# A hybrid decoder layer: the down projection in five groups instead of three, its product sums partly copied by ScalarE, and the first up pair in another order

## What is computed

```
h = h + xo @ p["w_xo"]
u, gv = jnp.split(rmsnorm(h, p["norm_ffn_g"]) @ p["w_up"], 2, axis=-1)
u, new_ffn_buf = causal_dwconv(u, ffn_buf, p["ffn_conv_w"])      # 3 taps
h = h + (jax.nn.silu(u) * gv) @ p["w_down"]
...
y_prompt = rmsnorm(hp, final_norm_g)
```

## Time and profile before

| quantity | value |
|---|---|
| time, median of 3 runs | 1997.17 us (1996.79 to 1999.99) |
| time of the profiled execution | 1992.7 us |
| its span | 1990.9 us |
| mean granted TensorE clock | 0.981 |
| PE, PEld busy | 1817.4 us (91%), 1699.2 us (85%) |
| DVE, ACT, POOL busy | 1206.2, 694.0, 748.6 us |
| first up product, first down product, end part | at 1227.12, 1704.83, 1951.93 us |

### The profile page before, as it was taken

One profiled execution on the slowest core, in us unless ns is written; L12 is line 12 of the kernel. 1 busy time (PEld: TensorE's weight loads), 2 busy tenths in 40 slices (PEclk: granted clock), 3 DMA queues, 4 the chain that ended last, 5 costly groups with the idle time before them and its releaser, 6 DMA issues. The chain is left out here.

```text
span 1990.9 us, 35520 instructions
## 1 busy us (share of the span) xinstructions
PE 1817.4 (91%) x14041; PEld 1699.2 (85%) x14041; DVE 1206.2 (61%) x1506; ACT 694.0 (35%) x1292; POOL 748.6 (38%) x621
## 2 busy tenths in 40 slices
PE   6988899999999899999999796999999999699997
PEld 5866799987887788998988596999999999698887
DVE  6877366754554231564142448788888888856655
ACT  6055326643222103412032526333333333424333
POOL 3411033331211123755664022444445454344444
PEclk9999999999999999999999998999999999799999
DMA  4311111110102021422222201332222332534422
GB/s 187 91 38 40 38 43 37 38 61 27 33 31 65 24 79 71 151 86 98 73 85 111 83 33 43 102 107 82 96 91 89 105 100 84 201 109 140 138 90 98
DMA packets 78242, 164.36 MB, mean 83 GB/s; under 512 B 7360, under 2 KB 28544, under 8 KB 76960
## 3 DMA queue, kind: packets, MB, share of 16 engines
q1 hardware_dynamic: 78128, 162.74, 24.4%
HBM read 125.11 MB, written 37.94 MB: 82 GB/s over the span
## 5 line engine op out<-in xcount | busy, mean ns | idle before, releaser
L696 PE MATMUL PS<-XH,WH 128*128 128x352 f32 x1224 | 275.5, 333 | 37.8 <-POOL WL L1040 14.0
L696 PE MATMUL PS<-XH,WL 128*128 128x352 f32 x1224 | 264.6, 324 | 0.0
L696 PE MATMUL PS<-XL,WH 128*128 128x352 f32 x1224 | 264.1, 324 | 0.0
L696 PEld LDWEIGHTS PS<-XH,WH 128*128 128x128 f32 x1224 | 208.0, 190 | 56.0 <-issue 35.6
L1048 POOL TENSOR_TENSOR WH<-RAW,CST 128x256 fp32r<-128x256 f32 x90 | 65.7, 757 | 483.2 <-PE PS L1818 196.1
L696 PEld LDWEIGHTS PS<-XH,WL 128*128 128x128 f32 x1224 | 210.6, 188 | 0.0
L696 PEld LDWEIGHTS PS<-XL,WH 128*128 128x128 f32 x1224 | 208.6, 189 | 0.0
L2462 PE MATMUL PS<-XH,WL 128*128 128x264 f32 x1296 | 169.4, 287 | 13.4 <-issue 13.4
L2462 PEld LDWEIGHTS PS<-XH,WL 128*128 128x128 f32 x1296 | 163.9, 190 | 13.7 <-issue 13.7
L1088 POOL TENSOR_TENSOR WL<-RAW,WL 128x512 fp32r<-128x512 f32 (+1 forms) x66 | 104.9, 1589 | 137.1 <-ACT WL L1603 135.4
L1038 POOL TENSOR_TENSOR WH<-RAW,CST 128x1024 fp32r<-128x1024 f32 x22 | 45.3, 2059 | 265.3 <-PE PS L696 139.7
(11 more groups left out here) (591 smaller groups left out, 4093.0 us busy)
## 6 DMA issues: line engine op xcount, KB each, us to landing
RAW<-in_w SPq DMA_DIRECT2D x70, 512.0 KB, 3.5
RAW<-in_wf SPq DMA_DIRECT2D x95, 256.0 KB, 2.6
TMP<-acts SPq DMA_DIRECT2D x70, 264.0 KB, 4.0
acts<-H SPq DMA_DIRECT2D x50, 264.0 KB, 2.1
RAW<-in_wf SPq DMA_DIRECT2D x28, 192.0 KB, 2.4
acts<-TMP SPq DMA_DIRECT2D x20, 264.0 KB, 2.1
H<-in_xT SPq DMA_DIRECT2D x4, 1056.0 KB, 9.0
TMP<-in_xT SPq DMA_DIRECT2D x2, 2112.0 KB, 8.3
```

Of the source, the lines that this page charges most:

```text
L696: mm = nc.tensor.matmul(PS[:, 3 * mm_g + c, 0:CW], w_[:, p, off + k * P:off + (k + 1) * P], x_[:, xk0 + k, c * CW:(c + 1) * CW], start=fir ...
```

## The change

1. `DOWN` has five groups of two k-blocks, (2, 0) to (2, 16), in place of three: 140 products of 12 matmuls, and 20 pairs instead of 12. A weight load of the down projection is 256 wide instead of 512 and 384, with 80 loads instead of 48.
2. `plan_units` gives every unit one of the zones' 28 slots and a product behind which it is made. A zone holds four k-blocks and a group needs two, so units of the next group are made through the whole group before (those of group 0 during the last up pair, those of group 1 from the second pair of group 0). There are 8 unit places, three of them in `EXTRA`, a new SBUF tensor of 7*528 columns. SP loads raw blocks and units of the late pairs product by product.
3. `on_pool` moves some unit rests to POOL: 6 of the first 14, then every third (L1151 after).
4. `down_copy` on ACT copies the sums of products 0, 1, 2 and 4 from PSUM to `EXTRA`; DVE adds from there (L3305 after), and PE waits for the copy (`d_cp`) in place of the read. Sums 3, 5 and 6 are still read from PSUM by DVE.
5. In every up pair, the fourth block sum (L3124 after) stands behind the read of product 4 instead of in front of it.
6. First up pair: the seven adds of squares go from DVE to POOL, with four buffers instead of two; ACT makes the first two weight heads within the loop over the inputs, DVE the first block sums two steps earlier; inputs of products 5 and 6 change places in ACT's and DVE's order; the matmuls on ones and Ln/Exp come one product later; `h_spill` is written in two parts and after the scaling; four of the eight scalings of `H` go to POOL, in the second up pair.

The diff, cut to what matters:

```diff
-DOWN = ((4, 0), (3, 8), (3, 14))
+DOWN = ((2, 0), (2, 4), (2, 8), (2, 12), (2, 16))
...
+def plan_units():
+    free = {(i, k): NP7 * (UPAIRS - 1) + i for i in range(NP7) for k in range(4)}
+    found = []
+    for g, (kh, f0) in enumerate(DOWN):
+        mine = [u for u in UNITS if u[0] == g]
+        for j, (_, i, k) in enumerate(mine):
+            slot = min(free, key=lambda x: (free[x], x))
+            if g == 0:
+                at_ = NP7 * (UPAIRS - 1) + j // kh
+            elif g == 1:
+                at_ = first_product(0) + NP7 + 3 * NP7 * j // len(mine)
+            else:
+                at_ = first_product(g - 1) + 4 * NP7 * j // len(mine)
+            used = free[slot]
+            found.append((slot, used, max(at_, used)))
+            free[slot] = first_product(g) + 3 * NP7 + i
...
+def on_pool(u):
+    return u % 5 in (1, 3) if u < 14 else u % 3 == 1
...
-        f_sq = [TMP[:, 0:T], TMP[:, T:2 * T]]
-        f_ss = TMP[:, 2 * T:3 * T]
+        f_sq = [TMP[:, 0:T], TMP[:, 5 * T:6 * T], EXTRA[:, 0:T], EXTRA[:, T:2 * T]]
+        f_ss = EXTRA[:, 2 * T:3 * T]
...
-        unit_place = [TMP[:, a:a + HT] for a in (0, HT, 1570, 1570 + HT, 2626)]
-        unit_place += [TMP[:, 5232 + HT * i:5232 + HT * i + HT] for i in range(4)]
-        assert R_AT + 4 * BLK <= 5232 and 5232 + 4 * HT <= 7 * T
+        unit_place = [EXTRA[:, HT * i:HT * i + HT] for i in range(3)]
+        unit_place += [TMP[:, a:a + HT] for a in (0, HT, 1570, 1570 + HT, 2626)]
+        d_copy = [EXTRA[:, HT * i:HT * i + HT] for i in range(3, 7)]
+        COPIED = (0, 1, 2, 4)
...
+            block_loads(1, 1)
+            sp.wait_ge(h_z, 1)
+            sp.dma_start(d["h_spill"][0], H[:, 4, :]).then_inc(h_in, 16)
+            sp.wait_ge(h_z, 4)
+            sp.dma_start(d["h_spill"][1:4].rearrange("k p t -> p k t"), H[:, 5:8, :]).then_inc(h_out, 16)
...
+            rest_split(NSLOTS - 2, 0)
+            ffn_add(1)
+            rest_split(NSLOTS - 1, 1)
+            for t in range(2, 6):
+                ffn_add(t)
+            pool.wait_ge(w_used, NSLOTS - 1)
+            block_rest(0, 0, 0)
+            ffn_add(6)
+            block_rest(1, 1, 0)
+            block_rest(2, 2, 0)
+            ffn_add(7)
+            for i in range(3, NP7):
                 block_rest(i, i, 0)
             for i in range(NP7):
                 block_rest(NP7 + i, i, 1)
-            with pool.Fori(1, FT // 2) as j:
+                if i in (1, 3, 5, 6):
+                    if i == 1:
+                        pool.wait_ge(h_z, 4)
+                        pool.wait_ge(fx_lo, 28)
+                    scale_h((1, 3, 5, 6).index(i))
...
+            for n in range(FT - 2, NPAIRS):
                 for i in range(NP7):
                     m = NP7 * n + i
                     block_rest(m, i, n % 2, block_width(n), block_source(i, n % 2))
+                    unit_rests(m - 5)
...
+                    if t == 7:
+                        head(1, 1, 0, 0)
...
+                if t == 5:
+                    head(0, 0, 0, 0)
...
+            def down_copy(n, i):
+                q = n - UPAIRS
+                j = COPIED.index(i)
+                act.wait_ge(q_mm, NP7 * n + i + 1)
+                if q:
+                    act.wait_ge(d_rd, D_RD + NP7 * (q - 1) + i + 1)
+                nc.scalar.activation(halves(d_copy[j]), sums(i, n % 2), ACT.Copy).then_inc(d_cp, 1)
...
+                        for s in ((), (), (0,), (1,), (2, 3), (4,), (5,))[i]:
...
-                        pe.wait_ge(d_rd, D_RD + NP7 * q + {2: 1, 3: 2, 4: 3, 6: 5}[i])
+                        pe.wait_ge(d_cp, D_CP + 4 * q + {2: 1, 3: 2, 4: 3, 6: 4}[i])
...
-                if part == 2 or part == 1 and not first:
+                if part == 2:
...
                 up_read(n, 4, p)
+                block_sums(n + 1, 1 - p, 2)
+                if isinstance(n, int) and n == 0:
+                    for k in range(4, 8):
+                        scale_h(k)
...
-                mlp_conv(n, p)
-                if isinstance(n, int) and n < 2:
-                    scale_h(2 * n)
-                    scale_h(2 * n + 1)
+                if not last:
+                    mlp_conv(n, p)
+                    mlp_gate(n, p, half)
...
+                src = sums(i, n % 2)
+                if i in COPIED:
+                    dve.wait_ge(d_cp, D_CP + 4 * d_ + COPIED.index(i) + 1)
+                    src = halves(d_copy[COPIED.index(i)])
+                nc.vector.tensor_tensor(h, h, src, ALU.add).then_inc(d_rd, 1)
             for n in range(UPAIRS, NPAIRS):
                 for i in range(NP7):
                     down_read(n, i)
-                    if n + 1 < NPAIRS and i in (0, 3):
-                        block_sums(n + 1, (n + 1) % 2, i // 3)
+                    if n + 1 < NPAIRS and i in (0, 2, 3):
+                        block_sums(n + 1, (n + 1) % 2, (0, 2, 3).index(i))
                     unit_rests(NP7 * n + i)
```

More of the change, by code:

```diff
@@ L891, in block_loads @@
                 base = NP7 * (n - 1)
-                if part == 0:
+                if x == "a11":
                     if first:
@@ L2486, in up_pe @@
                         ready = (lambda k: 5 * k + 1, lambda k: 5 * k + 2, lambda k: 5 * k + 4, lambda k: 5 * k + 3,
-                                 lambda k: 5 * k + 5, lambda k: 24 + k + 1, lambda k: 20 + k + 1)[i]
-                    product(NP7 * n + i, i, p, 4, NP7 * p + i, ready)
-                    if first and i == 1:
+                                 lambda k: 5 * k + 5, lambda k: 20 + k + 1, lambda k: 24 + k + 1)[i]
+                    x = [[z[:, k, :] for z in x_block(i)] for k in range(4)]
+                    product(NP7 * n + i, i, p, x, NP7 * p + i, ready)
+                    if first and i == 2:
                         pe.wait_ge(nadd, 28)
@@ L3156, in mlp_conv @@
                 for j in range(3):
+                    if between and j:
+                        between(j)
                     w_ = CST[:, bass.ds(CONST["ffn_w"][0] + 3 * t + j, 1)]
```

348 lines of the change are left out of this document (162 added, 186 removed).

## The result

| | before | changed |
|---|---|---|
| time, median (runs) | 1996.98 us (4) | 1980.32 us (4) |
| ratio to before | | 0.9927 (95%: 0.9904 to 0.9951) |
| profiled execution, span | 1990.9 us | 1976.3 us |

A forecast was written before the change was run, and what follows sets the result against it. TensorE, busy 91% of the span, was taken as the bound, so only its waits counted. Savings of 28.2 (down projection), 10.3 (up loop) and 13.0 (first up pair) made 51.5: 1997.2 to 1946 us, range 1928 to 1980.

The forecast's parts named there:

- Up loop: Up pairs: moving the fourth block sum behind the read removes 9.3 us of waits plus restarts, 10.3 saved (8 to 12).
- First up pair: Start of the up stage: earlier first product and second pair save 16.9 us, 3.9 given back, net 13 (4 to 20).
- second pair: Second up pair: 3.9 us given back, for the later H spill and GpSimd scaling four H blocks between weight rests.
- first pair: First up pair: after 4 us idle for the second product's weights, everything comes in time; second pair starts about 1242.5.
- Port in the down projection: Down pairs: VectorE and GpSimd exclude each other at SBUF; 0.4 us lost in each of 16 pairs, 6 (0 to 58).
- First change of group: First down pair: product 3 waits for ScalarE's copy behind the SiLU, 5.4 us, plus 1.1 for unit loads; 6.5 (4 to 14).
- Late loads and the restored `H`: Later group changes in the down projection: 2 us lost to late loads and reads of the restored H block.
- The copies: Down projection: ScalarE's copies from PSUM to SBUF give VectorE nothing, as one operation follows each copy.
- A (port, 1964): Rival: the shared port binds, down pairs take 11.3 to 12 us, some 18 us more, total 1964; chance 0.19.
- B (head, 1959): Rival: head of the up stage does not improve, H spill and GpSimd's adds cancel 13 us, total 1959; chance 0.11.

The follow-up runs named there:

- e4: Kernel before the change, with only the fourth block sum of each up pair moved behind the read of product 4: 1981.2 us, ratio 0.9941.
- e1: Changed kernel with the seven adds of squares back on VectorE at their former places: 1969.3 us, ratio 0.9874 to the kernel before.
- e2: Changed kernel with GpSimd's four scalings of H in the second up pair back on VectorE: 1970.64 us, ratio 0.988 to the kernel before.
- e9: Changed kernel with adds and scalings on VectorE, four H blocks saved unscaled and scaled after being read back: 1964.86 us, ratio 0.9847 to the kernel before.
- e15: e13 plus ScalarE making product 5's high input parts before the weight heads of products 3 and 4, first up pair: 1950.6 us, ratio 0.9782.
- e5: Changed kernel with GpSimd's unit rests behind the first 14 units back on VectorE: 1968.37 us, one run.
- combined kernel: Changed kernel with adds, scalings and later unit rests on VectorE, and the H restore behind the raw block: 1956.94 us, ratio 0.9807 to the kernel before.
- e8: Changed kernel with the last tile's SiLU behind the copies of products 1 and 2 in the first down pair: 1981.51 us, one run.
- e13: Combined kernel with copies of products 0 and 1 before unit heads and the SiLU behind copies at the first group change: 1952.45 us, ratio 0.9798.
- e7: Changed kernel with the load of the four saved H blocks issued behind the third down pair's raw block: 1978.7 us, one run.
- e12: Changed kernel with GpSimd's later unit rests on VectorE and without ScalarE's copies: 1985.08 us, one run.
- e6: Changed kernel without ScalarE's copies, VectorE adding all seven sums of a pair from PSUM: 1981.56 us, ratio 0.9938 to the kernel before.

## Why the prediction was wrong, step by step

- **Up loop, 10.3.** Right; 11.7 with the same line alone (e4). The waits were 9.28 of it; I had taken 0.1 for each restart where 0.24 was lost.
- **First up pair, 13.0 saved.** This is the step that failed first and the largest: A to C lost 12.2 instead, which is 25.2 of the 36.3 by which the stages miss the forecast. The sentence was "so VectorE wins little in the loop". I had the port rule, had scaled the add to 2.4 on GpSimd against 1.17, and then did not put the difference on VectorE's chain: 6 x 1.23 = 7.4. Measured: 6.9 (e1). With the adds away, the first product comes 43.7 behind the first `H` add; my 1216 is 43.4.
- **The same step, second pair.** I charged 3.9 for the late saving of `H` and the four scalings on GpSimd. The scalings alone cost 6.9 (e2), because they stretch the convolution, and ScalarE's SiLU and the read behind it wait for that; the four scalings on VectorE in one piece cost 5.5 more (e9), and I had not listed them as queued in front of the read of product 5, though they stand there in VectorE's order. Of the late saving of `H` no row shows a cost: ScalarE's reads in that pair wait for VectorE.
- **The same step, first pair.** "Then weights, inputs and the Ln come in time" was assumed, not worked out. They did not: 35.3 even without GpSimd's adds, where I had 26.5. ScalarE's order is 2.6 of it (e15); some 6 of the 8.8 stay open, among them the slow clock behind the waits (5.62 for a product of 2.92).
- **Port in the down projection, 6.** Measured 8.5 for the later unit rests on GpSimd alone (e5). The range given for the term, 0 to 58, held it. In the sixteen pairs from the fourth on, 9.5 is lost over 10.2 each; in the combined kernel, with these rests on VectorE, nothing is. I had VectorE's load as 7.1 a pair; its busy time is 217 in 20 pairs, 10.9 a pair of 11.6, but that counts the time for which its instructions are held up too, so it does not show by how much the 7.1 was off.
- **First change of group, 6.5.** The mechanism (a copy behind the SiLU in ScalarE's order) was right for the second wait. The first, 4.41 for the copy of product 0, was not in the forecast: that copy stands behind unit heads that wait for their loads, for which I had added 1.1. Idle was 8.07 and the slow clock behind the two waits 2.8 more, which I had not charged; the pair took 11.3 over 10.2. Behind these two the next copy in ScalarE's order holds PE (e8, e13).
- **Late loads and the restored `H`, 2.** Mis-sized as well: the third pair alone loses 4.6, where the loads issued behind the 2112 KB of the restore land only after it (e7). How much of the 4.6 they make is not shown: in e5, where VectorE waits 2.72 for the same load, the third pair loses 1.7 and the first 2.1 more than in the changed kernel.
- **The copies.** That "the copies give VectorE nothing" was right (it is busy for 217.2 in the stage with them, 186.3 without), and it was the wrong question: they let PE run ahead of VectorE (e12: 12.1; e6: 2.2), above all in the first two pairs.
- **Chances.** A (port, 1964) and B (head, 1959) were written as alternatives with 0.19 and 0.11. They are one mechanism in two places and came together, neither at its price: the head cost 25.2 instead of 13, and E came out 12.6 above its forecast, of which the port is 8.5 and not 18. So 1946 + 18 + 13 = 1977 comes within 4 of the time by luck. My range ended at 1980 because no case held both.

## What to carry to other kernels

Work given to GpSimd is not free when VectorE is on the path: as the first estimate, charge VectorE with GpSimd's whole duration for every tensor-tensor operation that runs beside its own SBUF operations, and move work there only if that is less than what VectorE saves. Here the same add cost the chain 2.05 of its 2.4 there and takes 1.17 at home. Rivals with one cause are not alternatives; add them up for the end of the range. And the cheapest edit, one block sum behind the read that TensorE waits for, gave as much as the whole change: before a rebuild of a stage, look for the instruction in front of the late one.

## What the runs showed of the hardware

The exclusion of VectorE and GpSimd reaches further than the two-input adds of the earlier trace rows. In stages A and C it also held for VectorE's scalar-tensor-tensor steps, which have two SBUF inputs too (0.76 alone and 3.09 beside GpSimd for 528 columns, 1.27 and 3.53 for 1024), and even for a copy of 16 columns within SBUF. That one takes 0.17 at its shortest; in the changed kernel it starts while a GpSimd scaling runs and ends with it, at 1264.37 and 1264.35:

```profile
1262.35 2.02 DVE L3194 COPY TMP<-TMP 128x16 f32<-128x16 f32 x1
...
1261.89 2.46 POOL L1120 TENSOR_TENSOR H<-H,TMP 128x1056 f32<-128x1056 f32 x1 [2.36 <-DVE H L3243]
```

The Trainium skill (SBUF — State Buffer, Who interferes with whom) calls the ports that the two engines share an exclusive lock. By that section a VectorE instruction with two SBUF inputs contends with a GpSimd one that reads SBUF, and a copy can do so in its two-port modes, for which whoever issues first has the ports for the whole instruction and the other blocks fully. The copy's row agrees, and the 2.05 for each add fits; I had used the shorter rule that the prediction cites, which has no amount. Who issued first can't be read from recorded starts as close as those of the rows at 1195.15 and 1268.11: VectorE's step starts 0.05 and 0.01 before GpSimd's add or scaling there, and it is VectorE's that is held up. The reads with a PSUM operand were never touched: 689 to 705 over 60 times, beside a GpSimd that was busy 177.5 of the 231.5 of the stage.

TensorE's granted clock in the changed kernel (the third last column of each stretch, a share of the full 2.4 GHz). TensorE had been idle for 4.41 in front of the first stretch; it is at the lower of its two levels there, 1.2 GHz, and its twelve matmuls take 3.01 instead of 1.62. Behind the idle 3.66 and one more such product it is back:

```profile
1713.30:1716.30 3.00, 2.99 (x12) 2.70 (x12) 3.00 (x3) 0.26 (x1) 3.00 (x3) 0.51 0.00 0
1722.80:1725.80 3.00, 3.00 (x25) 3.00 (x25) 3.00 (x6) 1.45 (x3) 1.31 (x2) 0.95 0.01 3
```

Behind the waits of 0.40, 0.66 and 1.50 in the kernel with the copies first, twelve matmuls took 1.70 to 1.73; behind one of 4.65 again 3.01.
